# Moving row shifts on the chip, spreading row maxima evenly and a fourth score bank in a gated attention block

## What is computed

```python
for blk in range(S // Q_BLOCK):                        # branch A ("fox"), 8 heads of 64
    logits = einsum('bqhd,bkhd->bhqk', q[:, qs:qe], k[:, :qe]) * scale
    logits = logits + F[:, :, qs:qe, None] - F[:, :, None, :qe]   # F: running sum of log sigmoid(f)
    logits = where(causal, logits, NEG_INF)
    outs.append(einsum('bhqk,bkhd->bqhd', softmax(logits), v[:, :qe]))
...
logits = einsum('bcqhgd,bcshd->bchgqs', qc, kb) * Dh ** -0.5      # branch B ("swa"), window of 2 chunks of 64
logits = logits - slopes * dist                        # and one learned sink per head in the softmax
...
x = x + gate * ((sigmoid(ga) * ya + sigmoid(gb) * yb) @ w_out)
```

## Time and profile before

| | us |
|---|---|
| median of 3 runs (2164.13 to 2168.77) | 2168.77 |
| the profiled execution, its time | 2172.97 |
| its span, from the first to the last instruction | 2171.2 |
| stages up to attend | 1098 |
| attend, first to last matmul | 658 |
| merge and output | 403 |

### The profile page before, as it was taken

One profiled execution on the slowest core, in us unless ns is written; L12 is line 12 of the kernel. 1 busy time (PEld: TensorE's weight loads), 2 busy tenths in 40 slices (PEclk: granted clock), 3 DMA queues, 4 the chain that ended last, 5 costly groups with the idle time before them and its releaser, 6 DMA issues. The chain is left out here.

```text
span 2171.2 us, 28183 instructions
## 1 busy us (share of the span) xinstructions
PE 2000.7 (92%) x9722; PEld 1560.1 (72%) x9722; DVE 890.2 (41%) x1850; ACT 749.9 (35%) x1439; POOL 555.6 (26%) x534
## 2 busy tenths in 40 slices
PE   7489999999999999999959999999989959998998
PEld 2368878788788788888846665665656639998887
DVE  2945555652211220000044554555645525654332
ACT  2622222220111312111127576677677751001100
POOL 0610000000000000000006575576667651210000
PEclk9589999999999999999969898999999989999999
DMA  6233333445411212121172445445454224322322
GB/s 232 97 100 100 114 118 95 140 129 119 122 67 68 73 56 87 52 83 68 48 172 63 105 111 116 108 95 134 106 128 106 67 86 148 116 97 97 107 97 78
DMA packets 230121, 222.98 MB, mean 103 GB/s; under 512 B 53586, under 2 KB 187730, under 8 KB 227444
## 3 DMA queue, kind: packets, MB, share of 16 engines
q1 hardware_dynamic: 218116, 181.74, 30.0%
q0 software_dynamic: 11648, 39.85, 5.8%
q10 hardware_dynamic: 256, 0.13, 0.0%
HBM read 149.58 MB, written 72.09 MB: 102 GB/s over the span
## 5 line engine op out<-in xcount | busy, mean ns | idle before, releaser
L1012 POOL TENSOR_TENSOR Pl<-PT,Ph 128x512 fp32r<-128x512 f32 (+2 forms) x382 | 419.6, 1118 | 244.1 <-ACT Ph L1147 226.4
L454 PE MATMUL pj<-hTh,Wh 128*128 128x512 f32 x768 | 299.4, 390 | 0.9 <-DVE Wl L646 0.4
L455 PE MATMUL pj<-hTl,Wh 128*128 128x512 f32 x768 | 298.8, 389 | 0.0
L456 PE MATMUL pj<-hTh,Wl 128*128 128x512 f32 x768 | 298.8, 389 | 0.0
L454 PE MATMUL pj<-Wh,hTh 128*128 128x512 f32 (+1 forms) x640 | 245.4, 384 | 22.8 <-DVE Wl L646 22.8
L365 POOL DMA_DIRECT2D wraw<-in_w_in x84 | 45.2, 538 | 855.3 <-DVE Wl L646 849.4
L1140 ACT ACTIVATE PT<-sc 128x512 f32<-128x512 f32 (+2 forms) x382 | 198.1, 519 | 127.8 <-PE sc L1080 51.6
L456 PE MATMUL pj<-Wh,hTl 128*128 128x512 f32 (+1 forms) x640 | 239.3, 374 | 0.0
L455 PE MATMUL pj<-Wl,hTh 128*128 128x512 f32 (+1 forms) x640 | 239.0, 373 | 0.0
L1147 ACT ACTIVATE Ph<-PT 128x512 fp32r<-128x512 f32 (+2 forms) x382 | 214.3, 561 | 12.2
L1234 DVE TENSOR_REDUCE part_max<-mx 128x1 f32<-128x512 f32 (+3 forms) x288 | 168.6, 597 | 91.4 <-PE mx L1037 90.0
(11 more groups left out here) (214 smaller groups left out, 3573.8 us busy)
## 6 DMA issues: line engine op xcount, KB each, us to landing
qk_scratch<-qThl SPq DMA_DIRECT2D x96, 256.0 KB, 2.8
wraw<-in_w_in POOLq DMA_DIRECT2D x88, 256.0 KB, 3.9
g_scratch<-st SPq DMA_DIRECT2D x64, 256.0 KB, 2.4
gt<-g_scratch SPq DMA_DIRECT2D x16, 1024.0 KB, 7.8
xin<-in_x POOLq DMA_DIRECT2D x16, 512.0 KB, 4.8
wada<-in_w_ada SPq DMA_DIRECT2D x8, 1024.0 KB, 7.4
z_scratch<-st SPq DMA_DIRECT2D x32, 256.0 KB, 2.4
Qb<-qk_scratch SPq DMA_DIRECT2D x32, 256.0 KB
```

What stands on the lines that cost most here:

```text
L454: nc.tensor.matmul(out, a_hi, b_hi, start=first, stop=False)
L455: nc.tensor.matmul(out, a_hi, b_lo, start=False, stop=False)
L456: return nc.tensor.matmul(out, a_lo, b_hi, start=False, stop=last)
L1012: pool.tensor_tensor(Pl[n % NPH][0:rows, 0:w], PT[n % NP][0:rows, 0:w], Ph[n % NPH][0:rows, 0:w].bitcast(F32), ALU.subtract).then_inc(low_ ...
```

## The change

Row items: the maxima of a block keep their 16 steps of lead, but the row item now always comes three steps after the last tile. Fox tiles are 1.05 steps apart and s tiles 1.5, and no more than two items stand in a step before the steps begin (START is now -20). Rows: SP's store and load through HBM are gone. One step after the transpose, ACT waits until DVE has written the row and issues the move from SBUF to SBUF itself (`move_row`), two DMAs for a fox row and four for an s row. Banks: four `sc` and two `mx` in place of three and three; AHEAD is 4; `PT`, `Ph` and `Pl` have five places in place of four. Keys: each of a head's two loads is cut into four of 512 keys, for heads 2 to 7 five steps apart. `set_up` and `tables()` run just before the first s tile and no longer after the first row item. The rest of the diff, left out here, renames semaphores and counts.

```diff
-    NSC, NMX, NP, NPH = 3, 3, 4, 4
+    NSC, NMX, NP, NPH = 4, 2, 5, 5
     VW, OUT = 2 * HD + 4, HD + 1
-    NQ, NZ = 4, 3
-    AHEAD = 3
-    TILE_LEAD, ROW_LEAD, SPACING = 16, 13, 0.8
+    NQ, NF, NZ = 4, 4, 3
+    AHEAD = 4
+    TILE_LEAD, ROW_LAG, SPACING, FIRST = 16, 3, {"f": 1.05, "s": 1.5}, -20
     timed = []
     for kind, starts in (("f", [(i, first["f", i]) for i in range(NB)]), ("s", [(t, first["s", 2 * t]) for t in range(TT)])):
         due = NS
         for i, start in reversed(starts):
-            row = min(start - ROW_LEAD, due)
-            due = min(start - TILE_LEAD, row)
-            timed.append((row, kind, i, None, None))
+            due = min(start - TILE_LEAD, due)
+            timed.append((due + ROW_LAG, kind, i, None, None))
             if kind == "f":
                 tiles = [(a, c) for a in range(JB) for c in range(i % JB + 1)]
             else:
                 tiles = [(g, half) for g in range(KV_H) for half in range(2)]
             for a, c in reversed(tiles):
                 timed.append((due, kind, i, a, c))
-                due -= SPACING
+                due -= SPACING[kind]
     timed = sorted(reversed(timed), key=lambda d: d[0])
-    items, at = [d[1:] for d in timed], [math.floor(d[0]) for d in timed]
+    items, at = [d[1:] for d in timed], [max(math.floor(d[0]), FIRST + u // 2) for u, d in enumerate(timed)]
     START = at[0]
     at_step = {n: [u for u, d in enumerate(at) if d == n] for n in range(START, NS)}
     item_no = {it: u for u, it in enumerate(items)}
+    SETUP = min(u for u, it in enumerate(items) if it[0] == "s") - 1
     row_item = lambda kind, i: item_no[kind, i, None, None]
     mx_after = lambda kind, i: row_item(kind, i) + 1
...
     row_step = lambda kind, i: at[row_item(kind, i)]
-    k_due = when((h, START + 9 * h if h < 2 else last["f", (h - 2) * JB + 3] - AHEAD + 1) for h in range(FOX_H))
+    k_due = when(((h, c), START + 9 * h if h < 2 else last["f", (h - 2) * JB + 3] - AHEAD + 1 + 5 * c) for h in range(FOX_H) for c in range(JB))
     q_due = when((i, START + 2 * i if i < NQ else last["f", i - NQ] - AHEAD + 1) for i in range(NB))
     v_due = when(((h, c), START + 3 + 2 * c if not h else last["f", h * JB - 1] - 15 + 4 * c + 4) for h in range(FOX_H) for c in range(JB))
     s_due = when((t, START + 1 + 7 * t if t < 2 else last["s", 2 * t - 3] + 1) for t in range(TT))
     z_due = when((e, START + 4 + 2 * e if e < NZ else last[blocks[e - NZ]] + 2) for e in range(NBLK))
-    row_store = when(((kind, i), row_step(kind, i) + 2) for kind, n in (("f", NB), ("s", TT)) for i in range(n))
-    row_load = when(((kind, i), row_step(kind, i) + 5) for kind, n in (("f", NB), ("s", TT)) for i in range(n))
+    row_move = when(((kind, i), row_step(kind, i) + 1) for kind, n in (("f", NB), ("s", TT)) for i in range(n))
...
-            def load_k(h):
-                u, rows = h % 2, slice(R_K + h * HD, R_K + (h + 1) * HD)
-                if h >= 2:
+            def load_k(h, c):
+                u, rows, cols = h % 2, slice(R_K + h * HD, R_K + (h + 1) * HD), slice(c * QW, (c + 1) * QW)
+                if h >= 2 and c == 0:
                     sp.wait_ge(scored, last["f", (h - 2) * JB + 3] + 1)
-                sp.dma_start(Ka[u][0:HD, :].bitcast(F32), dram["qk"][rows, 1, :]).then_inc(k_in[u], 16)
-                if h < 2:
-                    sp.wait_ge(cleared, (1, NQ + 2)[h])
-                sp.dma_start(Ka[u][HD:HD + 2, :].bitcast(F32), dram["f"][h]).then_inc(k_in[u], 16)
-
-            def load_k_pairs(h):
-                u, rows = h % 2, slice(R_K + h * HD, R_K + (h + 1) * HD)
-                sp.dma_start(Kb[u][:].bitcast(F32), dram["qk"][rows, :, :].rearrange("d s n -> (d s) n")).then_inc(kb_in[u], 16)
+                sp.dma_start(Ka[u][0:HD, cols].bitcast(F32), dram["qk"][rows, 1, cols]).then_inc(k_in[u], 16)
+                if c == 0:
+                    if h < 2:
+                        sp.wait_ge(cleared, (1, NQ + 2)[h])
+                    sp.dma_start(Ka[u][HD:HD + 2, :].bitcast(F32), dram["f"][h]).then_inc(k_in[u], 16)
+
+            def load_k_pairs(h, c):
+                u, rows, cols = h % 2, slice(R_K + h * HD, R_K + (h + 1) * HD), slice(c * QW, (c + 1) * QW)
+                sp.dma_start(Kb[u][:, cols].bitcast(F32), dram["qk"][rows, :, cols].rearrange("d s n -> (d s) n")).then_inc(kb_in[u], 16)
...
-            def store_rows(kind, i):
-                sp.wait_ge(mx_read, mx_after(kind, i))
-                if kind == "f":
...
-                else:
-                    sp.dma_start(dram["shift_b"][i], srow[i % 2].bitcast(F32)).then_inc(srow_out, 16)
-
-            def load_rows(kind, i):
-                if kind == "f":
-                    sp.wait_ge(frow_out, 16 * (i + 1))
-                    sp.dma_start(Qa[i % NQ][HD + 2:HD + 4, :].bitcast(F32), dram["shift_a"][i]).then_inc(q_in[i % NQ], 16)
-                else:
...
-                    for k in range(2):
-                        sp.dma_start(QBa[i % 2][HD + 2 * k:HD + 2 * k + 2, :, :].bitcast(F32),
-                                     dram["shift_b"][i, k * SWA_H:(k + 1) * SWA_H].rearrange("h s n -> s h n")).then_inc(s_in[i % 2], 16)
-
             for n in range(START, NS + TAIL):
                 if n == START + 1:
-                    sp.dma_start(sinks[:], io["swa_sinks"].to_broadcast([P, SWA_H])).then_inc(srow_out, 16)
-                for kind, i in row_load(n):
-                    load_rows(kind, i)
-                for kind, i in row_store(n):
-                    store_rows(kind, i)
-                for h in k_due(n):
-                    load_k(h)
+                    sp.dma_start(sinks[:], io["swa_sinks"].to_broadcast([P, SWA_H])).then_inc(sinks_in, 16)
+                for h, c in k_due(n):
+                    load_k(h, c)
                 for i in q_due(n):
                     load_q(i)
-                for h in k_due(n):
-                    load_k_pairs(h)
+                for h, c in k_due(n):
+                    load_k_pairs(h, c)
...
                     if x == "A" and g == 0:
-                        pe.wait_ge(s_in[t % 2], s_total(t) + 32)
...
+            def move_row(kind, i):
+                act.wait_ge(mx_read, mx_after(kind, i))
+                if kind == "f":
+                    for s in range(2):
+                        act.dma_start(Qa[i % NQ][HD + 2 + s:HD + 3 + s, :].rearrange("o (t n) -> o t n", n=P).bitcast(F32),
+                                      frow[i % NF][:, s, :].bitcast(F32)).then_inc(q_in[i % NQ], 16)
+                else:
+                    for k in range(2):
+                        for s in range(2):
+                            row = HD + 2 * k + s
+                            act.dma_start(QBa[i % 2][row:row + 1, :, :].bitcast(F32),
+                                          srow[i % 2][k * SWA_H:(k + 1) * SWA_H, s, :].bitcast(F32)).then_inc(s_in[i % 2], 16)
+
             for n in range(START, NS + 1):
+                for kind, i in row_move(n):
+                    move_row(kind, i)
                 for u in at_step.get(n, ()):
                     kind, i, a, c = items[u]
                     if a is None:
                         high_row(u)
-                        if (kind, i) == ("f", 0):
-                            tables()
                     elif kind == "s" and (a, c) == (KV_H - 1, 1):
                         act.wait_ge(sink_added, i + 1)
                         nc.scalar.activation(shift[:, i % 2, 1], shift[:, i % 2, 1], ACT.Exp).then_inc(sink_exp, 1)
+                    if u == SETUP:
+                        tables()
                 if 0 <= n + AHEAD < NS:
                     exp(n + AHEAD)
                     cast(n + AHEAD)
...
                 for u in at_step.get(n, ()):
                     take(u)
-                    if items[u] == ("f", 0, None, None):
+                    if u == SETUP:
                         set_up()
```

More of the change, by code:

```diff
@@ L859, in attend @@
         rows_ = sb("shift_rows", [P, 4, P], F32R)
-        frow = [rows_[32 * k:32 * k + JB, 0:2, :] for k in range(NQ)]
+        frow = [rows_[32 * k:32 * k + JB, 0:2, :] for k in range(NF)]
         srow = [rows_[32 * k:32 * k + 2 * SWA_H, 2:4, :] for k in range(2)]
@@ L870, in attend @@
         v_in, sum_out = [sem(f"a_v{k}") for k in range(JB)], [sem(f"a_so{k}") for k in range(NZ)]
-        frow_out, srow_out, inv_out, r_in = (sem("a_" + n) for n in ("frowo", "srowo", "invo", "r"))
+        sinks_in, inv_out, r_in = (sem("a_" + n) for n in ("sinks", "invo", "r"))
         init, ready, dist_ready, bias_ready = (sem("a_" + n) for n in ("init", "ready", "dist", "bias"))
@@ L877, in attend @@
         block = ctx.enter_context(nc.Block())
-        s_total = lambda t: 16 * sum((5 if x == 0 else 6) + 2 * (x < t) for x in range(t % 2, t + 1, 2))
+        s_total = lambda t: 16 * sum((5 if x == 0 else 6) + 4 * (x < t) for x in range(t % 2, t + 1, 2))
         s_off = lambda t: 0 if t else CHUNK
@@ L1030, in row_max @@
```

(12 more changed lines are left out.)

7 lines of the change are left out of this document (2 added, 5 removed).

## The result

The changed kernel takes 2200.55 us (median of 4 runs, 2197.53 to 2211.01) against 2167.16 us of the kernel before (4 runs, 2164.13 to 2168.77): a ratio of 1.0134 with a 95% interval of 1.0084 to 1.0184. It was wrong in its sign.

The account below looks back on a forecast made before the run. PE bounds, ACT second, each needing 64 us of a head's 79 to 85; ACT bounds after the change. Six heads -61.6, stretch before -8, last -2, start +12: -59.6, to 2109 us, range 2085 to 2150.

Parts of the forecast that it names:

- ACT's issues: On ACT's queue, 16 row-move issues a head at 0.3 us each add 4.8 us a head.
- dear issues: Rival: row-move issues on ACT cost 0.61 us each, a head takes 76 us, total 2147; chance 0.15.
- ACT as a whole became the bound: In each head, ACT's 64 us plus 5 for issues makes 69, more than PE's 64, so ACT bounds.
- The late rows: At s rows late from HBM, moves on the chip remove 12.6 us of PE waits and 25 us of lowered clock.
- The fold: Before the maxima's transposes, the later row item removes PE's 22.7 us of fold waits, 3 us a head.
- Queries late: Rival: queries for each head's fourth block, first tile, come 2 us late seven times; 26 us, total 2135; chance 0.08.
- an even pace: Evenly spaced maxima, with AHEAD 4 and five places, remove most of POOL's 9.2 us of waits, 1 to 1.5 a head.
- Two banks: Maxima banks: forecast counts nothing beyond 1.5 us a head; rival at 0.2 us an item gives 2185, chance 0.10.
- The start: Start of attend: table wait, key loads, extra items and two banks, less fold waits, lose 12 us (7 to 17).
- The clock: Late s rows drop PE's clock; with them gone it stays at 1.00 from about 1170 to the end of attend.
- The price of a head: In attend, a head falls from 79 to 85 us to 70.5: ACT's 69 plus 1.5 for the blocks' ends.
- The moves bring nothing: Rival: shared DMA engines hold the rows past 14 us, so row waits and clock loss stay; 2147, chance 0.04.

Follow-up runs that it names:

- the first three edits: Changed kernel with rows moved by SP, set-up and tables inside the wait for block 1's queries, s tiles 0.8 steps apart: 2156.01 us, 0.9919.
- clean kernel: Kernel of all three edits with three score and three maxima banks, AHEAD 3, then five query tiles and four PT, Ph, Pl places: 2122.38 us, 0.9746.
- the plan alone: Kernel before with only the item plan changed: row item three steps after the last tile, fox tiles 1.05 and s tiles 1.5 steps apart: 2158.98 us, 0.9906.

## Why the prediction was wrong, step by step

The forecast missed by 91 us. By the ratios, the first three edits together take back 47 of them, three banks each 8 (within the noise), the fifth query tile 30. The steps that failed are the price of ACT's issues, the s loads and the banks, which the forecast did not count, and the queries, which it took for unlikely.

**ACT's issues: the term that was mis-sized.** The prediction had both prices before it, 0.21 and 0.61 us, and took 0.3, since the row loads that the moves replace took 0.30 on SP. That was the nearest row by what is carried. The right one was the nearest by how it lies: L1168, also one row in several short pieces. Measured were 0.59 and 0.63. The price that follows was in the rival called dear issues: a head of 76. The clean kernel with the moves on ACT has 77.3, and the same kernel without them 72.3. That rival had the right price and the wrong time: its 2147 is still a gain, since it held every other term of the forecast. That ACT as a whole became the bound, as the prediction says, is not shown. In these six heads ACT itself waits 60.8 us for PE's scores; it is late where the moves stand, and idle elsewhere. Its sum of 64 us was also too high: only the four copies of s blocks are followed by a store of 0.61 us, the four of fox blocks by one of 0.21 (both in the earlier trace rows), so the eight copies with their stores take some 8 us and not 10.

**The late rows: right in mechanism, too large.** The moves remove every wait for a row in the middle of the stage. (They are issued 12 steps before the block, but its first scores are done 4 steps ahead of it, so the margin was 8 steps and not the 12 of the prediction; it was enough.) The prediction priced waits and clock at 38 us; alone they are worth 23, with an interval of 15 to 31. Against ACT's issues in the same kernel that is nothing left (1.0006).

**The fold: right, and more was won than shown in idle time.** No kernel with the row item three steps later waits for `nmax` by more than 0.2 us. Alone, the plan brings 20 us although it adds late queries with 10 us at half clock in six heads.

**Queries late: named as a rival, with a chance of 0.08.** The place, the fourth block's first tile, was right, but in the changed kernel itself the waits are only 0.5 to 1.2 us, three times. With all three edits, still at AHEAD 4, they are 1.0 to 2.1 us a head. The 30 us that five query tiles bring were measured at AHEAD 3, where the load has a step less: there it has 2.3 us and takes 5.3 (1210.54, 1212.81 and 1215.87 above), against the 5.5 us that the prediction gave it. So the 26 us of the rival and these 30 are not the same quantity, and what the fifth tile is worth with four score banks was not tried. Three things can make the wait longer: shorter heads, one step less of AHEAD, and the moves in SP's list. No run tests one of them by itself.

**The s loads: missing.** The prediction spoke of the spacing of s tiles only as part of an even pace. That the first of four tiles goes ahead by 2.1 steps, while the release of what it reads does not, is arithmetic on the plan, and it was not done. It cost 27 us in the changed kernel. The spacing is not the only condition: the plan alone in the kernel before had no such wait with the same spacing, and the kernel before with the rows moved on the chip had some with a spacing of 0.8 and whole keys. Why is not shown.

**Two banks: priced at nothing, and at 75 us as a rival.** Neither holds. It is 23 us in the clean kernel (some 9 to 37 by the two intervals), 0.06 us for each of 378 items. In the forecast it should have stood as a term of its own.

**The start: +12 predicted, +18 measured.** The wait for the tables was put at 8 us and is 8.47. The queries of block 1 came later too: before, its first tile was at 1120.00, after at 1125.89, 1.4 of it from the later start of the stage. In SP's list three more key loads take 1.73 us and four `Kb` 2.36, where one took 0.43, all ahead of these queries. PE stands 10.0 us there and not 6.83, though the profile names no releaser for this wait. Some 5 us of the 18 are not taken apart:

```profile
1113.62 0.80 PE L1016 MATMUL mx<-Ka,Qa 66*128 66x128 f32 x2 [14.13 <-DMA Qb<-qk_scratch]
...
1125.89 0.87 PE L1016 MATMUL mx<-Ka,Qa 66*128 66x512 f32 x2 [10.03 <-issue]
...
1140.72 0.55 PE L1025 MATMUL mx<-biasM,identr 128*128 128x256 f32 x1 [8.47 <-ACT biasB L1110]
```

**The clock: right that late loads drop it, wrong that nothing else would.** Removing a wait of 2 us brings the clock back only if no other loss takes its place. Here the falls stand at the s loads and at the waits for an `ot` bank, and three of 6.8 us (at 1280, 1440 and 1604) where PE has only waited for POOL, twice 0.7 us.

**The price of a head: reached by another kernel, and in part by luck.** The prediction had 64 us a head from PE's columns, which no kernel here tests, and 70.5 from ACT's sum with the moves on it. With the moves off ACT, three banks each, the s tiles close and five query tiles a head takes 71 to 72.5 us, and the whole kernel 0.9746 of before, which on 2168.77 us is 2114. The predicted time was that of a kernel with five further edits, with the moves off the engine from whose sum it had been worked out; that the numbers meet does not bear that sum out.

**The moves bring nothing, by the rule of the Trainium skill** (page "DMA: Bandwidth & Descriptors", section "Issuing engines are not separate DMA queues": what another engine as issuer saves is issue time alone). As a rival it fell: the rows do come in time on either queue, though with ACT's issues the kernel before is no faster for it (1.0006). The trace adds the other side of the sentence: the issue time, 0.6 us each, is taken from the engine that issues, and on ACT exponentials that PE needs stand behind it.

The prices of single edits do not add up. Against the clean kernel the changed one has ACT's issues (39 us), four query tiles (30) and two banks (23); with the s loads (27) and the tables (9) that is 128, while by the two ratios the changed kernel is 3.9% or 84 us above it. The sum of five such differences is uncertain by some 30 us. Beyond that I take it for stalls that overlap, each hiding part of the next; the fourth score bank and the fifth places, whose gain was not measured by itself, are in it too.

## What to carry to other kernels

Price a DMA that is moved to a computing engine by a row of the same form (inside SBUF, so many short pieces), not by the row of the DMA that it replaces, and then add it to that engine's own sum before comparing with the bound: here 16 issues of 0.6 us a head on ACT, with its 62 to 64 us of 80, cost 25 to 39 us more than on SP. On the issuing queue that has time, see what stands behind them all the same: on SP they held up keys and queries by 1.4 us. When a plan makes its consumer earlier, list for each load the step of its release and the step of its first reader, before and after; for queries and s tiles that distance shrank, from four or five steps to one and from nine to seven, and the tables lost the wait that had hidden them. When a gain is to come from several stalls going at once, the margins that were hidden behind them become the next stalls, and one more buffer (here the fifth query tile, 30 us) can be worth more than the change itself.

## What the runs showed of the hardware

- A move inside SBUF of a row in four or eight pieces costs its issuing engine 0.59 to 0.63 us, on ACT and on SP alike; a store of one piece costs ACT 0.21, and the load of a row from HBM cost SP 0.26 (medians). The queue does not matter, the form does. SBUF as a source does not set it alone, since the store of 0.21 has it too, nor do pieces, since an s row's load of 0.26 (L954) gathered eight for each row; which property does stays open.
- In the granted clock of the records, each of six waits of PE of 3.05 to 4.03 us (queries, the plan alone) goes with 10.2 us at 1.2 GHz, but one of 3.01 us (queries, the moves on SP) with 6.8. Waits of 1.6 to 2.6 us go with anything from nothing (1.65 us, the clean kernel) over 3.4 and 6.8 to 10.2 (2.14 us, all three edits). Of the short ones no rule came out: in the clean kernel waits of 1.04 and 0.98 us left the clock at 2.4 GHz, and with the moves on ACT it fell to 1.2 for 6.8 us in five of six heads, where no wait in the middle was over 1.0 us.
